# Scan decays: the running sums' rows fetched from memory as broadcasts and masked by GpSimd, instead of being spread and masked by matmuls

## The chip, the cores and the metric

The kernel runs on one core of a Trainium2 chip. The metric is the device time of one execution in microseconds (us), lower is better; three executions of the kernel before gave a median of 1445.81 us.

## The reference, cut to what matters

The kernel is one inference step of a two-layer backbone in float32. Layer 0 has differential attention beside a bidirectional state-space scan (SSD); layer 1 has a pooling mixer; both end in an MLP of width 4096. The change touches the scan of layer 0 alone. For one direction and one chunk of q = 128 tokens it computes

```python
acs = jnp.cumsum((dt * a).reshape(nb, nc, q, H), axis=2)
seg = acs[:, :, :, None, :] - acs[:, :, None, :, :]
causal = jnp.tril(jnp.ones((q, q), bool))[None, None, :, :, None]
decay = jnp.where(causal, jnp.exp(jnp.where(causal, seg, 0.0)), 0.0)
cb = jnp.einsum('bclhn,bcshn->bclsh', ch, bh) * decay
y_diag = jnp.einsum('bclsh,bcshp->bclhp', cb, xdt)
```

There are 5 chunks (4 of the 512 latent tokens, 1 of the 128 prompt tokens), 2 directions and 8 heads in 2 groups. The backward direction uses the opposite triangle.

## The kernel before, in words

The program is written engine by engine; semaphores are the only order between engines. Every engine runs its own list strictly in order, so an instruction that waits holds back all that stands behind it on that engine. Matmuls in the big projections are split into high and low halves (three products for one).

The part that matters is the loop `for j in range(2 * NT)` of layer 0, ten rounds, here called rounds 0 to 9. Each round of TensorE (PE) holds, in this order: one projection of 24 matmuls (`project_in`, L801), the decay matmuls (`decays`, L1008 and L1010), two transposes of a query or key block (`turn_qk`, L949), in even rounds 8 matmuls of a modulation product (`site`, L832), the products of the weighted pairs of the round before with the values (`chunk_y(j - 1)`, L1031), and the pair products C·B of this round (`pair_products(j)`, L1020). A pair u is one chunk and one group of four heads: u = 0 to 9.

For a pair u the decays are made so. The cumulated sums `acs` were transposed once to rows and multiplied with a small pick matrix into `acsr` (L2206). PE writes, for each direction, a bank of 128 x 512: first the triangle mask (0 or -1e30, from `maskr`, four times side by side, L1008), then it adds the rows of `acsr`, spread over all 128 partitions by a picking matmul (L1010). ScalarE (ACT) takes eight exponentials of 128 x 128 from PSUM, with the other sum as bias, into `seg[u % 2]` (L1541). VectorE (DVE) adds the two directions (L2158) and multiplies with the pair products (L2161, `weigh_pairs(u)`, semaphore `m_ok`). PE's `chunk_y(u)` waits for that; its end is the semaphore `yd_mm`.

DVE's list in round j is: `weigh_pairs(j - 1)`, `evac_in` of this round's projection (L2125 and L2134, or copies), in rounds 3 and 9 the low half of the next weight block (`split_lo`, L1926), in even rounds from 2 on `chunk_sum` (L2167, L2170). PE's first projection after the loop waits for the `split_lo` of round 9. GpSimd (POOL) has nothing to do in these rounds: it waits for the last `evac_in` to store two outputs (L645). It issues many of the kernel's DMAs and does small powers (L617, L720, L727).

Earlier, at the start, POOL loads small tables (L625 to L629, `ssd_c` holds the two triangles and the two masks, L628); ACT waits for all five, copies them (L1487 to L1490) and only then evacuates the first convolution input (L1507).

## Time and profile before

| | |
|---|---|
| median of 3 runs | 1445.81 us (1445.0 to 1446.02) |
| span of the profiled execution | 1442.8 us |
| PE busy | 1397.0 us (97%) |
| DVE busy | 1040.2 us (72%) |
| ACT busy | 543.1 us (38%) |
| POOL busy | 77.3 us (5%) |

The span is that of the one profiled execution, first to last instruction; the median of the timed runs lies 3.0 us above it. Busy time of PE is pipelined: a matmul of 256 columns is shown with about 280 ns although the next one starts 120 ns later, so what a group of matmuls costs is read from the starts of the groups, not from the busy time.

### The profile page before, as it was taken

To read this page: it belongs to the slowest core of one execution; us is meant where nothing else is said; L and a number is where in the kernel's file an instruction comes from. 1 tells how busy PE (TensorE), PEld (TensorE's weight loads), DVE (VectorE), ACT (ScalarE), POOL (GpSimd) and SP (SyncE) were. 2 spreads that over 40 slices of the span, in tenths; PEclk is the share of its full clock that TensorE was granted. 3 is DMA by queue.
4 is the path that set the end of the run, shared out by engine and by line. 5 is a ranking of instruction groups with operands and counts; after the bars stand their busy time and mean duration, and the time that the engine had idled before them with its cause. 6 is when DMAs were issued, how large, how long until landed. Compare 5 with 4: busy or idle time off the path is not lost.

```text
span 1442.8 us, 22837 instructions
## 1 busy us (share of the span) xinstructions
PE 1397.0 (97%) x8806; PEld 1240.1 (86%) x8806; DVE 1040.2 (72%) x1651; ACT 543.1 (38%) x982; POOL 77.3 (5%) x146
## 2 busy tenths in 40 slices
PE   4999999999999999999999999999999999999996
PEld 3899988766779998998899879888999889989985
DVE  3694566777568876776776796877887677667778
ACT  4333343367454332332232254434443223223322
POOL 1300000010201000000000111001000000000011
PEclk9999999999999999999999999999999999999998
DMA  9701234696713312321221723551332122123141
GB/s 316 232 30 60 88 118 133 213 310 228 265 45 137 126 59 83 94 87 59 87 88 58 268 88 114 185 185 37 146 103 85 62 88 88 59 87 116 59 160 73
DMA packets 132300, 177.47 MB, mean 123 GB/s; under 512 B 4170, under 2 KB 104258, under 8 KB 131698
## 3 DMA queue, kind: packets, MB, share of 16 engines
q1 hardware_dynamic: 123250, 146.46, 31.4%
q0 software_dynamic: 7376, 26.76, 5.3%
q10 hardware_dynamic: 1584, 3.01, 0.6%
q8 instruction: 61, 1.00, 0.3%
q14 instruction: 29, 0.24, 0.0%
HBM read 166.94 MB, written 9.27 MB: 122 GB/s over the span
## 4 chain that ended last, share of the span: by engine, by line
PE 79%; DVE 10%; ACT 5%; issue 2%; DMA 2%; SPq 1%; POOL 0%; ACTq 0%; DVEq 0%
PE ps L801 40%; PE ps L1325 20%; PE ps L783 5%; PE ps L792 4%; PE ps L832 2%; DVE convT L2024 2%; PE ps L1133 2%; DVE wlo L1926 1%; ACT h_full L1722 1%; SPq L570 1%; DVE p_pad L2691 1%; DMA raw_more<-in_w_mod_l 1%; ACT tmp L1722 1%; ACT whi L1430 1%; PE ps L1144 1%
## 5 line engine op out<-in xcount | busy, mean ns | idle before, releaser
L1430 ACT ACTIVATE whi<-raw 128x512 fp32r<-128x512 f32 (+2 forms) x193 | 178.6, 935 | 357.8 <-PE ps L801 293.6
L801 PE MATMUL ps<-whi,hid_hi 128*128 128x512 f32 x640 | 249.6, 390 | 0.0
L801 PE MATMUL ps<-wlo,hid_hi 128*128 128x512 f32 x640 | 249.2, 389 | 0.0
L801 PE MATMUL ps<-whi,hid_lo 128*128 128x512 f32 x640 | 249.1, 389 | 0.0
L1926 DVE TENSOR_TENSOR wlo<-raw,whi 128x512 fp32r<-128x512 f32 (+2 forms) x193 | 204.9, 1070 | 26.0 <-ACT whi L1430 22.5
L2357 DVE TENSOR_TENSOR acc<-acc,ps 128x512 f32<-128x512 f32 x120 | 80.2, 684 | 122.0 <-PE ps L801 122.0
L801 PE MATMUL ps<-whi,h_hi 128*128 128x256 f32 (+1 forms) x480 | 157.4, 328 | 2.5 <-DVE wlo L1926 1.4
L801 PE MATMUL ps<-whi,h_lo 128*128 128x256 f32 (+1 forms) x480 | 152.9, 319 | 0.0
L801 PE MATMUL ps<-wlo,h_hi 128*128 128x256 f32 (+1 forms) x480 | 152.8, 318 | 0.0
L801 PEld LDWEIGHTS ps<-whi,hid_hi 128*128 128x128 f32 x640 | 120.1, 188 | 25.4 <-DVE wlo L1926 0.8
L801 PEld LDWEIGHTS ps<-whi,hid_lo 128*128 128x128 f32 x640 | 120.1, 188 | 25.1
L801 PEld LDWEIGHTS ps<-wlo,hid_hi 128*128 128x128 f32 x640 | 120.1, 188 | 24.2
L1325 PE MATMUL ps<-t_hi,whi 128*128 128x320 f32 x384 | 118.7, 309 | 0.0
L1325 PE MATMUL ps<-t_hi,wlo 128*128 128x320 f32 x384 | 118.7, 309 | 0.0
L1325 PE MATMUL ps<-h_lo,whi 128*128 128x320 f32 x384 | 118.6, 309 | 0.0
L1325 PE MATMUL ps<-h_hi,whi 128*128 128x320 f32 x384 | 118.2, 309 | 0.0
L2497 DVE TENSOR_TENSOR tmp<-tmp,ps 128x320 f32<-128x320 f32 x168 | 79.2, 483 | 37.2 <-PE ps L1325 33.1
L801 PEld LDWEIGHTS ps<-whi,h_hi 128*128 128x128 f32 x480 | 91.2, 190 | 10.3 <-DVE wlo L1926 2.0
L801 PEld LDWEIGHTS ps<-whi,h_lo 128*128 128x128 f32 x480 | 91.2, 190 | 6.5
L801 PEld LDWEIGHTS ps<-wlo,h_hi 128*128 128x128 f32 x480 | 91.4, 190 | 5.9
L1325 PE MATMUL ps<-h_hi,wlo 128*128 128x320 f32 x288 | 89.0, 309 | 0.0
L783 PE MATMUL ps<-h_hi,whi 128*128 128x320 f32 x320 | 73.4, 310 | 0.0
(339 smaller groups left out, 2654.6 us busy)
## 6 DMA issues: line engine op xcount, KB each, us to landing
raw<-in_w_up_l SPq DMA_DIRECT2D x32, 1024.0 KB, 5.6
raw<-in_w_down_l SPq DMA_DIRECT2D x32, 1024.0 KB, 4.9
raw<-in_w_mod_l SPq DMA_DIRECT2D x26, 1024.0 KB, 5.8
raw<-in_w_in_l SPq DMA_DIRECT2D x12, 1024.0 KB, 5.2
raw_split<-in_w_mod_l SPq DMA_DIRECT2D x8, 1024.0 KB, 6.7
raw<-in_w_out_l SPq DMA_DIRECT2D x6, 1024.0 KB, 5.9
x_spill<-x_tok POOLq DMA_DIRECT2D x10, 512.0 KB, 2.9
x_tok<-x_spill POOLq DMA_DIRECT2D x10, 512.0 KB, 6.2
```

What stands on the lines that cost most here:

```text
L783: mm = pe.matmul(outs[hf], w_of(still, k), a_of(part, k, hf), start=(k == 0 and part == 0 and still == 0), stop=(k == nk - 1 and still == 1))
L792: mm = pe.matmul(out, w_of(still, k), a_of(part, k, hf), start=(k == 0 and part == 0 and still == 0), stop=(k == nk - 1 and still == 1))
L801: mm = pe.matmul(out, a_of(still, k), w_of(part, k), start=(first and k == 0 and part == 0 and still == 0), stop=(last and k == nk - 1 and ...
L832: mm = pe.matmul(ps[32 * g:32 * g + 32, lo:lo + BW], cpad[:, k, :], raw_block(mod_k[m])[:, k * BW:(k + 1) * BW], start=(k < 4), stop=(k >= 4))
L1133: mm = pe.matmul(bank(2 * n + part, 0, keys.shape[-1]), qT[r:r + DH, 2 * n + hp, t * P:(t + 1) * P], keys, start=True, stop=True)
L1325: mm = pe.matmul(bank(b, 0, HALF), WP[still][:, pos // 4, lo:lo + P], moving(part, k), start=(k == 0 and still == 0 and part == 0), stop=( ...
L1430: act.activation(ring_piece(whi, w, g), piece(w, g), ACT.Copy).then_inc(hi_done, 1)
L1722: ins = act.activation(dst, bank(TURN[i % 2][t][f // 4], (f % 4) * P, (f % 4 + 1) * P), ACT.Identity, bias=modT[:, layer, q, f, c:c + 1], ...
L1926: dve.tensor_tensor(ring_piece(wlo, w, g), piece(w, g), ring_piece(whi, w, g).bitcast(F32), ALU.subtract).then_inc(lo_done, 1)
L2024: ins = dve.scalar_tensor_tensor(dst, src, tap, dst, ALU.mult, ALU.add)
L2357: dve.tensor_tensor(dst, dst, bank(4 + g % 4), ALU.add).then_inc(acc_ok, 1)
L2497: dve.tensor_tensor(dst, a, bank(b, 0, HALF), ALU.add).then_inc(comb, 1)
```

## The change

The four decay matmuls of each round, the masks in `maskr`, the pick matrices and `acsr`'s product are gone. In their place the transposed sums (one transpose and one copy, `acsr` is now 80 x 128) are stored once to memory (`acs_rows`). POOL fetches for each pair the four rows of each direction, broadcast to all 128 partitions, straight into `seg[u % 3]` (512 KB, now three buffers), and puts -1e30 outside the triangle with one `affine_select` of 128 x 512 for each direction (semaphore `tri_ok`). ACT then takes the same eight exponentials in place, from `seg` and no longer from PSUM. The table `t_ssd` shrinks from four to two blocks of 128 x 128, so its load and ACT's copy of it are half as large, and the copy of the identity is gone. DVE has five small instructions less at the sums and one copy for two products.

```diff
+            def fetch_rows(u):
+
+                first = 8 * ORDER[u // 2] + 4 * (u % 2)
+                if u >= 3:
+                    pool.wait_ge(yd_mm, u - 2)
+                rows = A["acs_rows"][:, first:first + 4, :].rearrange("d h n -> d (h n)")
+                pool.dma_start(seg[u % 3][:].rearrange("p d h n -> p d (h n)"), rows.partition_broadcast(P)) \
+                    .then_inc(seg_ld[u % 3], 16)
+
+            def triangle(u):
+
+                pool.wait_ge(seg_ld[u % 3], 16 * (u // 3 + 1))
+                for d in range(2):
+                    side = 1 - 2 * d
+                    pool.affine_select(seg[u % 3][:, d], seg[u % 3][:, d], [[0, 4], [side, P]], ALU.is_ge, NEG,
+                                       base=0, channel_multiplier=-side).then_inc(tri_ok, 1)
+
+            pool.wait_ge(acs_ok, 4)
+            pool.dma_start(A["acs_rows"].rearrange("d h n -> (d h) n"), acsr[0:80]).then_inc(rows_st, 16)
+            pool.wait_ge(rows_st, 16)
+            for u in range(2):
+                fetch_rows(u)
+            for u in range(2 * NT):
+                if u + 2 < 2 * NT:
+                    fetch_rows(u + 2)
+                triangle(u)
...
-            def decays(u):
-
-                c, g = ORDER[u // 2], u % 2
-                for d in range(2):
-                    if u >= 1:
-                        pe.wait_ge(eexp, 2 * (u - 1) + d + 1)
-                    else:
-                        pe.wait_ge(acs_ok, 3)
-                        pe.wait_ge(xb_ev, KT)
-                    pe.matmul(bank(d), maskr[:, 4, :], maskr[:, 2 + d, :].unsqueeze(1).to_broadcast([P, 4, P]),
-                              start=True, stop=False)
-                    pe.matmul(bank(d), pickr[0:80, 2 * c + g:2 * c + g + 1].to_broadcast([80, P]), acsr[0:80, d, :],
-                              start=False, stop=True).then_inc(r_mm, 1)
...
-            act.activation(maskr[:, 0:4, :], ssdc[:], ACT.Copy)
-            act.activation(maskr[:, 4, :], ident, ACT.Copy).then_inc(mask_ok, 1)
+            act.activation(maskr[:], ssdc[:], ACT.Copy).then_inc(dt_w, 1)
...
             def decays(u):
 
                 c, g = ORDER[u // 2], u % 2
-                if u >= 2:
-                    act.wait_ge(yd_mm, u - 1)
                 for d in range(2):
-                    act.wait_ge(r_mm, 2 * u + d + 1)
+                    act.wait_ge(tri_ok, 2 * u + d + 1)
                     for h in range(4):
-                        ins = act.activation(seg[u % 2][:, d, h, :], bank(d, h * P, (h + 1) * P), ACT.Exp,
+                        ins = act.activation(seg[u % 3][:, d, h, :], seg[u % 3][:, d, h, :], ACT.Exp,
                                              bias=nacs[:, d, c, 4 * g + h:4 * g + h + 1])
                     ins.then_inc(eexp, 1)
```

How the built programs stand, at the two places that matter. First POOL's list between the loads of the start and the stores of outputs, before; `kc`, `rope_t`, `state_ld` and `v_tok` are loads of the start, `out` are stores:

```order
L635 DMA rope_t_98<-in_t_rope 128x256
L637 DMA state_ld_111<-in_state_ssm_l0 128x4x128 x2
L640 DMA v_tok_90<-in_cache_v_l0 128x512 x2
L645 DMA out_2<-tmp_67 128x256 x2
L647 DMA out_3<-v_tok_90 128x512
```

The same place in the changed program; `acs_rows_102` is the tile, `acs_rows` the tensor in memory, and seg0, seg1 and seg2 are the three buffers:

```order
L632 DMA state_ld_109<-in_state_ssm_l0 128x4x128 x2
L635 DMA v_tok_90<-in_cache_v_l0 128x512 x2
L656 DMA acs_rows<-acs_rows_102 80x128
L644 DMA seg0_104<-acs_rows 128x2x512
L644 DMA seg1_105<-acs_rows 128x2x512
L644 DMA seg2_106<-acs_rows 128x2x512
L652 ISA
L652 AFFINE_SELECT seg0_104<-seg0_104 128x512 x2
L644 DMA seg0_104<-acs_rows 128x2x512
L652 AFFINE_SELECT seg1_105<-seg1_105 128x512 x2
L644 DMA seg1_105<-acs_rows 128x2x512
L652 AFFINE_SELECT seg2_106<-seg2_106 128x512 x2
```

The fetch into a buffer stands ahead of the selects of another buffer: the fetch of pair 3 (second row of seg0's DMA) waits for `chunk_y(0)`, and behind it stand the selects of pair 1, and so on in every round.

Second, PE's list in round 2, before, from the end of the projection to the first matmuls of the next:

```order
L801 MATMUL ps<-whi_57,h_lo_61 128x256
L1008 MATMUL ps<-mask_r_100 128x512
L1010 MATMUL ps<-acs_rows_102,pick_r_105 128x512
L1008 MATMUL ps<-mask_r_100 128x512
L1010 MATMUL ps<-acs_rows_102,pick_r_105 128x512
L949 MATMUL ps<-head_68,tmp_67 128x128 x2
L832 MATMUL ps<-raw_49,cpad_69 32x256 x8
L1031 MATMUL ps<-xb_tok_99,seg1_108 128x64 x4
L1020 MATMUL ps<-convT_86 128x128
L801 MATMUL ps<-whi_57,h_hi_60 128x256
```

And in the changed program:

```order
L822 MATMUL ps<-whi_57,h_lo_61 128x256
L970 MATMUL ps<-head_68,tmp_67 128x128 x2
L853 MATMUL ps<-raw_49,cpad_69 32x256 x8
L1035 MATMUL ps<-xb_tok_99,seg1_105 128x64 x4
L1024 MATMUL ps<-convT_86 128x128
L822 MATMUL ps<-whi_57,h_hi_60 128x256
```

The four decay matmuls are gone; all else on PE keeps its place.

## Rows read from the trace of the kernel before

**Rows 1.** The page: busy time of PE, and the chain by engine.

```profile
PE 1397.0 (97%) x8806; PEld 1240.1 (86%) x8806; DVE 1040.2 (72%) x1651; ACT 543.1 (38%) x982; POOL 77.3 (5%) x146
PE 79%; DVE 10%; ACT 5%; issue 2%; DMA 2%; SPq 1%; POOL 0%; ACTq 0%; DVEq 0%
```

**Rows 2.** Busy time by stretch: stretch, length, engines, granted clock, DMA share, GB/s.

```profile
169.50:221.40 51.90, 51.90 (x436) 46.03 (x435) 31.23 (x70) 27.05 (x88) 0.00 (x0) 1.00 0.38 122
20.00:30.00 10.00, 6.12 (x77) 3.08 (x76) 6.53 (x16) 6.00 (x9) 0.00 (x0) 1.00 1.10 348
```

**Rows 3.** Timeline of PE in rounds 1, 8, 9: start, duration, what.

```profile
174.99 0.39 PE L1008 MATMUL ps<-mask_r 128*128 128x512 f32 x1
175.94 0.38 PE L949 MATMUL ps<-head,tmp 128*128 128x128 f32 x2
176.16 1.00 PE L1031 MATMUL ps<-xb_tok,seg 128*128 128x64 f32 x8
...
216.94 1.10 PE L1031 MATMUL ps<-xb_tok,seg 128*128 128x64 f32 x8
...
222.20 1.00 PE L1031 MATMUL ps<-xb_tok,seg 128*128 128x64 f32 x8
...
228.93 1.10 PE L1031 MATMUL ps<-xb_tok,seg 128*128 128x64 f32 x8
```

**Rows 4.** Timeline of ACT, round 0.

```profile
171.18 2.17 ACT L1541 ACTIVATE seg<-ps,ssd_small 128x128 f32<-128x128 f32 x8
```

**Rows 5.** Timeline of DVE, rounds 0 to 9, in brackets its wait before.

```profile
173.38 0.69 DVE L2158 TENSOR_TENSOR seg<-seg 128x512 f32<-128x512 f32 x1 [2.37 <-ACT seg L1541]
174.11 0.69 DVE L2161 TENSOR_TENSOR seg<-seg,ps 128x512 f32<-128x512 f32 x1
...
180.35 0.75 DVE L2125 TENSOR_TENSOR tmp<-ps,rope_t 128x256 f32<-128x256 f32 x2
181.13 0.49 DVE L2134 TENSOR_TENSOR tmp<-tmp 128x128 f32<-128x128 f32 x2
181.87 0.69 DVE L2167 TENSOR_TENSOR y_tok<-xb_tok,dsk 128x512 f32<-128x512 f32 x1 [0.24 <-DVE tmp L2134]
...
222.30 2.29 DVE L1926 TENSOR_TENSOR wlo<-raw,whi 128x2048 fp32r<-128x2048 f32 x1 [0.24 <-DVE tmp L2118]
```

**Rows 6.** Groups of POOL: busy time, mean ns of one, idle before.

```profile
L740 POOL DMA_DIRECT2D x_tok<-x_spill x10 | 5.2, 529 | 651.0 <-PE ps L1325 651.0
L622 POOL MEMSET conv_raw<- 128x1296 f32 x1 | 1.2, 1178 | 11.2 <-DVE cpad L1979 11.2
L605 POOL MEMSET cpad<- 128x256 f32 x1 | 0.3, 311 | 0.3 <-POOLq L2749 0.3
```

**Rows 7.** Timeline of POOL beside DVE, at the norms of layer 0.

```profile
412.25 0.69 DVE L2346 SCALAR_TENSOR_TENSOR x_tok<-x_tok,gated 128x512 f32<-128x512 f32 x1
...
412.36 0.63 POOL L727 TENSOR_TENSOR ln_small<-ln_small 128x1 f32<-128x1 f32 x1
415.47 0.19 POOL L727 TENSOR_TENSOR ln_small<-ln_small 128x1 f32<-128x1 f32 x1
```

**Rows 8.** The chain that ended last, pieces in order of time.

```profile
47.11 1.04 PE ps L832 x16
48.44 0.91 POOL wdt L625
...
51.25 5.44 DMA dsk<-in_d_skip_l
57.12 0.52 ACT mask_r L1489
```

**Rows 9.** Timeline of ACT at the table copies.

```profile
57.03 0.61 ACT L1489 ACTIVATE mask_r<-ssd_c 128x512 fp32r<-128x512 f32 x1
57.55 0.29 ACT L1490 ACTIVATE mask_r<-head 128x128 fp32r<-128x128 f32 x1
57.75 0.42 ACT L1507 ACTIVATE conv_raw<-ps 128x320 f32<-128x320 f32 x1
```

**Rows 10.** DMA issues: size of one, median us to landing.

```profile
x_tok<-x_spill POOLq DMA_DIRECT2D x10, 512.0 KB, 6.2
ln_gb<-in_ln_b_l POOLq DMA_DIRECT2D x4, 512.0 KB, 9.4
```

More of the change, by code:

```diff
@@ L234, in build @@
         cdec = rend
-        seg = [at(f"seg{n}", kb, [P, 2, 4, P]) for n, kb in enumerate((172, 186))]
+        seg = [at(f"seg{n}", kb, [P, 2, 4, P]) for n, kb in enumerate((172, 186, 168))]
         kc = at("kc", 176, [P, 2, 2, 4, DH])
@@ L293, in build @@
             ("xb_mm", "xb_ev", "cv_v", "cv_th", "cv_ok"))
-        ld_dt, ld_kc, ld_st, v_ev, mask_ok = (sem(n) for n in
-            ("ld_dt", "ld_kc", "ld_state", "v_ev", "mask_ok"))
+        ld_dt, ld_old, v_ev = (sem(n) for n in ("ld_dt", "ld_cache_state", "v_ev"))
         dt_w, dt_wl, dt_row, dt_cp, dt_mm, dt_v, dt_ok = (sem(n) for n in
@@ L301, in build @@
             ("xt_tr", "xt_ev", "acs_mm", "acs_ok", "kc_tr", "kc_ev", "sld_tr", "hst_ok"))
-        r_mm, g_mm, eexp, m_ok, yd_mm, y_ok = (sem(n) for n in
-            ("r_mm", "g_mm", "e_exp", "m_ok", "yd_mm", "y_ok"))
-        dec_s, dec_e, w_ok, off_mm, st_mm, off_ok, h_ok = (sem(n) for n in
-            ("dec_s", "dec_e", "ws_ok", "off_mm", "st_mm", "off_ok", "hs_ok"))
+        rows_st, g_mm, eexp, tri_ok, m_ok, yd_mm, y_ok = (sem(n) for n in
+            ("acs_rows_st", "g_mm", "e_exp", "triangle_ok", "m_ok", "yd_mm", "y_ok"))
+        seg_ld = [sem(f"seg_ld{n}") for n in range(3)]
+        dec_e, w_ok, off_mm, st_mm, off_ok, h_ok = (sem(n) for n in
+            ("dec_e", "ws_ok", "off_mm", "st_mm", "off_ok", "hs_ok"))
         nst_tr, nst_ev, yg_ok, yg_sq, yg_rs, yn_ok = (sem(n) for n in
@@ L982, in turn_sums @@
                 pe.wait_ge(acs_ok, 1)
-                for d in range(2):
-                    mm = pe.transpose(ps[0:80, 7 * 512 + 256 + P * d:7 * 512 + 256 + P * (d + 1)],
-                                      achl[:, d, :].bitcast(F32), ident)
-                mm.then_inc(acs_mm, 1)
+                pe.transpose(ps[0:80, 7 * 512 + 256:7 * 512 + 256 + P], sm[:, 80:160], ident).then_inc(acs_mm, 1)
             todo = [M_MIX]
@@ L997, in site @@
                     site_product()
-            def decays(u):
-                c, g = ORDER[u // 2], u % 2
-                for d in range(2):
-                    if u >= 1:
-                        pe.wait_ge(eexp, 2 * (u - 1) + d + 1)
-                    else:
-                        pe.wait_ge(acs_ok, 3)
-                        pe.wait_ge(xb_ev, KT)
-                    pe.matmul(bank(d), maskr[:, 4, :], maskr[:, 2 + d, :].unsqueeze(1).to_broadcast([P, 4, P]),
-                              start=True, stop=False)
-                    pe.matmul(bank(d), pickr[0:80, 2 * c + g:2 * c + g + 1].to_broadcast([80, P]), acsr[0:80, d, :],
-                              start=False, stop=True).then_inc(r_mm, 1)
             def pair_products(u):
@@ L1030, in chunk_y @@
                     cols = slice((4 * g + h) * DH, (4 * g + h + 1) * DH)
-                    mm = pe.matmul(bank(3, cols.start, cols.stop), seg[u % 2][:, 0, h, :], xb[:, ORDER[n], cols],
+                    mm = pe.matmul(bank(3, cols.start, cols.stop), seg[u % 3][:, 0, h, :], xb[:, ORDER[n], cols],
                                    start=True, stop=True)
@@ L2086, in _ @@
             settle()
[L2087 to L2093 removed]
+            dve.wait_ge(acs_ok, 1)
             mark(dve.tensor_tensor(dtw, rend, acs, ALU.subtract))
@@ L2097, in _ @@
             settle()
-            dve.nop().then_inc(dec_s, 1)
+            dve.nop().then_inc(acs_ok, 1)
             def evac_in(g):
@@ L2204, in _ @@
                     dve.wait_ge(acs_mm, 2)
-                    for d in range(2):
-                        ins = dve.tensor_tensor(acsr[0:80, d, :].rearrange("p (h n) -> p h n", h=4),
-                                                ps[0:80, 7 * 512 + 256 + P * d:7 * 512 + 256 + P * (d + 1)]
-                                                .unsqueeze(1).to_broadcast([80, 4, P]),
-                                                pick[0:80, 10:14].unsqueeze(2).to_broadcast([80, 4, P]), ALU.mult)
-                        if d == 0:
-                            mark(ins)
-                    ins.then_inc(acs_ok, 1)
+                    dve.tensor_copy(acsr[0:80], ps[0:80, 7 * 512 + 256:7 * 512 + 256 + P]).then_inc(acs_ok, 1)
             for j in range(2 * NT):
```

43 lines of the change are left out of this document (14 added, 29 removed).

## The prediction, made before the changed kernel ran

> **What bounds the kernel now.** I read the page first: PE is busy 97% of the span and makes up 79% of the chain that ended last [rows 1]. Then the busy time by stretch: from 169.5 to 221.4 us, which is the loop that the change edits but for its last round, PE is busy 51.90 of 51.90 us at a granted clock of 1.00, the 2.4 GHz level, while DVE is busy 31.2, ACT 27.1 and POOL not at all [rows 2]. So a microsecond taken from PE's list there is a microsecond of the kernel, until something else ends last. Last I read the timeline for the pace of the rounds and for what lies between one `chunk_y` and the next.
>
> **The rounds before.** The decay matmuls of a round take 175.94 - 174.99 = 0.95 us on PE [rows 3]. `chunk_y(0)` starts at 176.16 and `chunk_y(7)` at 216.94, seven rounds of 5.83 us on the mean; `chunk_y(8)` follows at 222.20 and `chunk_y(9)` at 228.93 [rows 3]. If nothing but PE mattered, ten times 0.95 us would go, 9.5 us.
>
> **What the new order makes of it.** POOL's list decides. Behind the fetch for pair u + 2 stand the selects of pair u, and that fetch waits for `chunk_y(u - 1)`, because it overwrites the buffer that this one reads. The selects of pair u need nothing from `chunk_y(u - 1)`, yet cannot pass the fetch. So for u = 1 to 7 there is a closed loop: `chunk_y(u - 1)`, issue of a fetch, select, eight exponentials, two DVE products, `chunk_y(u)`. Before, the exponentials of pair u ran while PE worked on the same round, ahead of `chunk_y(u - 1)`; two buffers let them. Fetches 8 and 9 are the last ones, so the selects of pairs 8 and 9 follow at once.
>
> One turn of the loop, from start to start of `chunk_y`:
> - `chunk_y` itself 1.00 [rows 3];
> - PE's end to POOL's start 0.29: the modulation product ends at 47.11 + 1.04 = 48.15 and POOL starts at 48.44 [rows 8];
> - issue of the fetch 0.57: a 512 KB load is issued in 0.53 [rows 6], a little more for two pieces per partition;
> - the first select, T (below);
> - to ACT 0.10, an estimate like the small gaps around it;
> - eight exponentials 2.17 [rows 4]; the last four need the second select, which is hidden while T is under 1.04 (half of 2.17, less the pipeline's tail);
> - to DVE 0.04 and the two products 1.42: 171.18 + 2.17 = 173.35, start 173.38, end 174.11 + 0.69 = 174.80 [rows 4, 5];
> - to PE 0.10, an estimate.
>
> Without T this is 5.69 us. It is already 0.14 short of a round of before.
>
> **The select.** No row has one. A memset takes 311 ns for 256 elements of a partition and 1178 for 1296 [rows 6]: 0.83 ns an element and 0.10 us fixed. At that rate 512 elements take 0.53 us, which is the bound below, since a select also reads, counts an index and compares. I take two such rates, 0.95 us. Three rates give 1.38 and four 1.81; above that no row leads. GPSIMD Engine Reference, section 3.1, of the Trainium skill gives 1.8 cycles at 1.2 GHz per element for a tight loop and 2.6 with two inputs; the estimate from that page would be 0.77 to 1.11 us for 512 elements, and the sum below would change by -1.3 to +1.6 us. No row here shows such a loop.
>
> **Seven turns.** L = 5.69 + 0.95 = 6.64 us. `chunk_y(0)` starts two decay groups earlier, at 176.16 - 1.90 = 174.26; its exponentials are not late, since both first fetches have 20 us. `chunk_y(7)` then starts at 174.26 + 7 x 6.64 = 220.74 in place of 216.94: **+3.8 us**. PE idles some 1.5 to 2.5 us in every round.
>
> **DVE in POOL's way.** An operation of POOL that reads a tile was held while DVE ran one with two tile inputs: the same L727 takes 0.19 us alone and 0.63 beside L2346, and ends 0.05 after it [rows 7]. The Trainium skill has it as a rule (SBUF — State Buffer, section "SBUF: two separate sides"): the two share a port pair, one that starts first keeps it for the whole instruction. The trace agrees, with that 0.63. Here the select of pair u would start 0.10 + 1.00 + 0.29 + 0.57 = 1.96 us after `m_ok` of the pair before. DVE runs `evac_in` until 1.3, and after a settle of 0.24 the L2167 of even rounds from 1.54 to 2.23 [rows 5]: 0.27 us in each of rounds 2, 4 and 6, 0.8 in all. In round 3 `split_lo` of 2.29 us stands there, from 1.54 to 3.83 [rows 5]: 1.87 us once. Together **+2.7 us**; nothing, if selects are not held.
>
> **The end of the loop.** Round 8 has selects that wait for nothing, so PE goes at its own pace: 5.26 - 0.95, and some 0.2 of waiting, 4.5 us in place of 5.26 [rows 3]. Behind `chunk_y(8)` the pair's DVE work is now late and `split_lo` of round 9 with it: from `m_ok` on some 0.85 for `evac_in` (two copies here, an estimate; 1.27 at most, as in round 2 [rows 5]), 0.24, 2.29, and from the end of `split_lo` to `chunk_y(9)` the 228.93 - 224.59 = 4.34 of before [rows 3, 5]; less the 0.1 from `m_ok` to `chunk_y(8)` that is 7.6 us in place of 228.93 - 222.20 = 6.73. Sum of both **+0.1 us**.
>
> **The start.** The chain runs through the table loads: the last of them lands 5.44 us after its issue, ACT copies, and DVE's convolution follows [rows 8]. ACT's two mask copies take 57.75 - 57.03 = 0.72 us [rows 9]. Afterwards one of 256 columns is left, about 0.31: **-0.4 us**. The halved table may save a little of the landing (0 to 0.3). The one transpose less at the sums is **-0.1 us** of PE. DVE's saved products (some 2 us) lie in rounds where DVE waits for PE: nothing.
>
> **What costs nothing while its cover holds.** A fetch is issued two turns, 13 us, ahead of its select; loads of 512 KB from POOL land in 6.2 to 9.4 us [rows 10], at a DMA share of 0.38 [rows 2]. If they took 16, each turn would grow by about 1.5 us, and the loop would be 10 us longer. The state transposes that now wait for one semaphore less were not late. The granted clock stayed at 1.00 in a stretch where PE was busy 6.12 of 10 us [rows 2], so idling a third of a round should leave it.
>
> **Sum.** 3.8 + 2.7 + 0.1 - 0.4 - 0.1 = +6.1 us. On the profiled execution's own 1442.8 that is 1448.9. The median of the runs lies 3.0 above that span; the same shift gives 1445.8 + 6.1 = **1451.9 us**.
>
> **Rivals.**
> - *The select is long* (T over 1.04). Then the second select sets the exponentials and L = 4.65 + 2T. At three memset rates that is 7.41, `chunk_y(7)` at 226.1, +9.2 in the loop and about +11.5 in all, 1457.3 us; at four rates 8.27 and 1463.3. For it: the select does at least three things where memset does one. Against it: it is one input and one output.
> - *No change.* T is 0.53 and selects are not held: L = 6.22, seven turns end at 217.8, +0.9, less 0.4 at start, end and sums: 1446.3 us. For it: memset's rate. Against it: the held L727.
> - *Faster.* The loop closes, but the exponentials read a tile instead of PSUM and follow each other faster: a copy of 128 x 128 from a tile is followed by the next instruction after 0.20 us [rows 9], an exponential now after about 0.26 [rows 4]. Eight of them save 0.46 a turn. With T = 0.53 and no holding L is 5.76 and the kernel takes 1443.0 us. Without holding, the sign turns at L = 6.15. Full PE pace, 4.9 us a round and 1435.8, would need another 0.9 us off every turn.
> - *A fetch that lands late*, as above: about 1462 us. Against it: 13 us of lead.
>
> **How the numbers follow.** Chances: the loop with a select of 0.53 to 1.04 us and held selects 0.55, the long select 0.21, no change 0.14, faster 0.07, late fetches 0.03. A measurement of this kernel can tell 0.2%, 2.9 us. The two slow rivals and the forecast make slower 0.79; "no change" is same, 0.14; faster is 0.07. The forecast's own span is 1449.0 (T 0.53, held) to 1452.5 (T 1.04, held); the range reaches down to the no-change case and up to a select of nearly four rates: 1445.5 to 1461.
>
> **What would show it.** In the changed profile: L1008 and L1010 gone; PE idle before L1035 in rounds 2 to 8 with DVE's `m_ok` product as releaser, 1 to 3 us each; starts of L1035 6.6 us apart instead of 5.2 and 6.4 in turn; the largest gap in round 4, behind `split_lo`'s round; POOL waiting for L1035 ahead of each fetch; the select's own length; none of PE's idle time released by a DMA. I am wrong if rounds are 4.3 and 5.3 us long (then something lets the selects run ahead), if selects take 0.5 us and don't care about DVE, or if they take over 1.4.

## The result, and the profile of the changed kernel

The changed kernel takes 1455.09 us in the median of four runs (1453.82 to 1456.1). The kernel before, run beside it, takes 1445.4 us (four runs, 1443.83 to 1446.02). The ratio is 1.0069, with an interval of 1.0057 to 1.0081: slower by 9.7 us. The profiled execution has a span of 1454.2 us, against 1442.8.

The page of the changed kernel, busy time and chain, as in [rows 1]:

```profile
PE 1397.4 (96%) x8765; PEld 1242.0 (85%) x8765; DVE 1039.8 (72%) x1645; ACT 545.5 (38%) x981; POOL 99.5 (7%) x177
PE 74%; DVE 10%; issue 6%; ACT 5%; DMA 2%; SPq 1%; POOL 1%; ACTq 0%; DVEq 0%; POOLq 0%
```

PE has 41 matmuls less, yet is shown busy as long as before, and its share of the chain fell from 79% to 74%. The busy time by stretch says why, over the same stretch as in [rows 2], then over the rest of the loop, one piece of it, and a piece of layer 1. The columns are stretch, length, busy time of PE, PEld, DVE, ACT and POOL, granted clock, DMA share, GB/s:

```profile
169.50:221.40 51.90, 41.97 (x332) 38.29 (x322) 25.45 (x56) 23.59 (x74) 16.41 (x23) 0.88 0.53 171
221.40:242.00 20.60, 17.82 (x139) 15.79 (x139) 12.67 (x24) 10.56 (x28) 3.34 (x6) 0.88 0.54 170
...
218.00:221.00 3.00, 3.00 (x16) 3.00 (x16) 0.00 (x0) 1.06 (x4) 2.47 (x4) 0.50 0.31 85
1000.00:1040.00 40.00, 37.30 (x224) 34.56 (x224) 29.12 (x47) 23.90 (x51) 3.78 (x7) 0.96 0.25 80
```

Where PE was busy 51.90 of 51.90 us at a clock of 1.00, it is now busy 41.97 us, at 0.88. Both are losses: PE waits, and part of what it does runs at the lower level, 1.2 GHz, which is the 0.50 of the third row.

The timeline of PE, all starts of `chunk_y` but three, with PE's wait before in brackets (in the changed file `chunk_y` is L1035, the projection L822):

```profile
173.55 1.02 PE L1035 MATMUL ps<-xb_tok,seg 128*128 128x64 f32 x8
180.25 1.10 PE L1035 MATMUL ps<-xb_tok,seg 128*128 128x64 f32 x8 [1.31 <-DVE seg L2153]
187.03 1.10 PE L1035 MATMUL ps<-xb_tok,seg 128*128 128x64 f32 x8 [2.31 <-DVE seg L2153]
...
216.25 1.97 PE L1035 MATMUL ps<-xb_tok,seg 128*128 128x64 f32 x8 [2.68 <-DVE seg L2153]
224.71 1.10 PE L1035 MATMUL ps<-xb_tok,seg 128*128 128x64 f32 x8
229.02 1.00 PE L1035 MATMUL ps<-xb_tok,seg 128*128 128x64 f32 x8
...
232.41 0.39 PE L822 MATMUL ps<-whi,h_hi 128*128 128x256 f32 x1 [2.11 <-DVE wlo L1924]
...
238.20 1.10 PE L1035 MATMUL ps<-xb_tok,seg 128*128 128x64 f32 x8
```

I call turn k the time from the start of `chunk_y(k-1)` to that of `chunk_y(k)`. The nine turns are 6.70, 6.78, 8.16, 6.77, 7.14, 7.15, 8.46, 4.31 and 9.18 us. Before, the first seven made 40.78 and the last two 11.99 us [rows 3]; now they make 51.16 and 13.49.

One turn through the engines, timelines of POOL, ACT and DVE. L644 is the fetch, L652 the two selects, L1539 the eight exponentials, L2150 and L2153 the two products:

```profile
174.87 0.73 POOL L644 DMA_DIRECT2D seg<-acs_rows  x1 [17.62 <-PE ps L1035]
175.61 1.24 POOL L652 TENSOR_SCALAR_AFFINE_SELECT seg<-seg 128x512 f32<-128x512 f32 x2
```

```profile
176.30 0.70 ACT L1539 ACTIVATE seg<-seg,ssd_small 128x128 f32<-128x128 f32 x2 [2.17 <-POOL seg L652]
...
177.78 0.97 ACT L1539 ACTIVATE seg<-seg,ssd_small 128x128 f32<-128x128 f32 x3
```

```profile
178.78 0.69 DVE L2150 TENSOR_TENSOR seg<-seg 128x512 f32<-128x512 f32 x1 [3.97 <-ACT seg L1539]
179.51 0.69 DVE L2153 TENSOR_TENSOR seg<-seg,ps 128x512 f32<-128x512 f32 x1
```

Read in order of time, each link starts within 0.1 us of the end of the one that it needs, from `chunk_y(0)` (ends 174.57) to `chunk_y(1)` (180.25), except POOL's start, 0.30 behind PE's end: issue to 175.60, first select (half of 1.24) to 176.23, exponentials to 178.75, products to 180.20. But for the second select, which runs under the first exponentials, nothing in this circle overlaps with anything else in it. The waits of the loop, in total, times, longest, give the same circle:

```profile
POOL seg L644 <- PE ps L1035: 47.7, 7, 17.6
ACT seg L1539 <- POOL seg L652: 26.4, 7, 4.7
DVE seg L2150 <- ACT seg L1539: 25.8, 8, 4.9
...
PE ps L1035 <- DVE seg L2153: 9.8, 5, 2.7
```

Last, the two places where POOL and DVE met: round 3 with `split_lo` (L1924), and round 6 with L2159, which takes 0.69 us elsewhere, as L2167 did in [rows 5]:

```profile
188.41 2.29 DVE L1924 TENSOR_TENSOR wlo<-raw,whi 128x2048 fp32r<-128x2048 f32 x1 [0.24 <-DVE tmp L2126]
...
210.62 1.16 DVE L2159 TENSOR_TENSOR y_tok<-xb_tok,dsk 128x512 f32<-128x512 f32 x1 [0.24 <-DVE tmp L2129]
```

```profile
189.17 2.62 POOL L652 TENSOR_SCALAR_AFFINE_SELECT seg<-seg 128x512 f32<-128x512 f32 x2
...
211.24 1.62 POOL L652 TENSOR_SCALAR_AFFINE_SELECT seg<-seg 128x512 f32<-128x512 f32 x2
```

Two selects take 1.24 us alone, 2.62 beside `split_lo` and 1.62 in round 6, where the DVE product beside them is 0.47 longer as well.

### The profile page after: what moved, and what is told of

It reads as the page before. It is cut to its first block, busy times and chain, and to the rows that moved or that the text cites. A ratio compares the mean times of both kernels' runs of the same rounds, so it can differ in the third digit from the quotient of the medians.

```text
span 1454.2 us, 22789 instructions
## 1 busy us (share of the span) xinstructions
PE 1397.4 (96%) x8765; PEld 1242.0 (85%) x8765; DVE 1039.8 (72%) x1645; ACT 545.5 (38%) x981; POOL 99.5 (7%) x177
## 4 chain that ended last, share of the span: by engine, by line
PE 74%; DVE 10%; issue 6%; ACT 5%; DMA 2%; SPq 1%; POOL 1%; ACTq 0%; DVEq 0%; POOLq 0%
PE ps L822 37%; PE ps L1326 20%; PE ps L804 5%; PE ps L813 4%; PE ps L853 2%; DVE convT L2022 2%; PE ps L1134 2%; DVE wlo L1924 1%; ACT h_full L1720 1%; SPq L565 1%; DVE p_pad L2676 1%; DMA raw_more<-in_w_mod_l 1%; ACT tmp L1720 1%; ACT whi L1431 1%; PE ps L1145 1%
## 5 line engine op out<-in xcount | busy, mean ns | idle before, releaser
L822 PE MATMUL ps<-whi,hid_hi 128*128 128x512 f32 x640 | 249.6, 390 | 0.0
L822 PE MATMUL ps<-wlo,hid_hi 128*128 128x512 f32 x640 | 249.1, 389 | 0.0
L822 PE MATMUL ps<-whi,hid_lo 128*128 128x512 f32 x640 | 249.1, 389 | 0.0
L1924 DVE TENSOR_TENSOR wlo<-raw,whi 128x512 fp32r<-128x512 f32 (+2 forms) x193 | 204.9, 1070 | 26.0 <-ACT whi L1431 22.5
L822 PE MATMUL ps<-whi,h_hi 128*128 128x256 f32 (+1 forms) x480 | 160.4, 334 | 2.9 <-DVE wlo L1924 2.4
L822 PE MATMUL ps<-whi,h_lo 128*128 128x256 f32 (+1 forms) x480 | 155.6, 324 | 0.0
L822 PE MATMUL ps<-wlo,h_hi 128*128 128x256 f32 (+1 forms) x480 | 155.5, 324 | 0.0
L822 PEld LDWEIGHTS ps<-whi,hid_hi 128*128 128x128 f32 x640 | 120.1, 188 | 25.3 <-DVE wlo L1924 0.8
L822 PEld LDWEIGHTS ps<-whi,hid_lo 128*128 128x128 f32 x640 | 120.1, 188 | 25.2
L822 PEld LDWEIGHTS ps<-wlo,hid_hi 128*128 128x128 f32 x640 | 120.2, 188 | 24.2
L822 PEld LDWEIGHTS ps<-whi,h_hi 128*128 128x128 f32 x480 | 94.3, 197 | 10.8 <-DVE wlo L1924 3.0
L822 PEld LDWEIGHTS ps<-whi,h_lo 128*128 128x128 f32 x480 | 94.0, 196 | 6.5
L822 PEld LDWEIGHTS ps<-wlo,h_hi 128*128 128x128 f32 x480 | 94.4, 197 | 5.8
```

Of the source, the lines that this page charges most:

```text
L822: mm = pe.matmul(out, a_of(still, k), w_of(part, k), start=(first and k == 0 and part == 0 and still == 0), stop=(last and k == nk - 1 and ...
L1924: dve.tensor_tensor(ring_piece(wlo, w, g), piece(w, g), ring_piece(whi, w, g).bitcast(F32), ALU.subtract).then_inc(lo_done, 1)
```

## The experiments

Each stands against the kernel before, run beside it. Where an experiment edits the kernel after, its time is also compared with that kernel's 1455.1 us.

### Fetch one pair ahead: is it the loop?

If the selects of pair u stand behind the wait for `chunk_y(u - 2)` and not for `chunk_y(u - 1)`, there is no closed loop of one round, with the same instructions and buffers.

```diff
-            for u in range(2):
+            for u in range(3):
                 fetch_rows(u)
             for u in range(2 * NT):
-                if u + 2 < 2 * NT:
-                    fetch_rows(u + 2)
+                if 3 <= u + 1 < 2 * NT:
+                    fetch_rows(u + 1)
                 triangle(u)
```

> Edit: GpSimd fetches only one pair ahead inside the loop, so the selects of pair u stand behind the wait for chunk_y(u-2), not behind the one for chunk_y(u-1). Nothing is left out. Theory A (a closed loop: the selects of a pair are issued behind the wait for the pair before it, and every round hangs on chunk_y, fetch issue, selects, exponentials, products): the loop is cut, the rounds go at TensorE's own pace of 4.3 and 5.3 us, no idle time over 0.5 us is left ahead of L1035 in the middle of the loop, the granted clock there is 1.00, and the time is 1435 to 1438 us (ratio to before 0.993 to 0.995). Theory B (the chain of a round is too long in any order, or the landing of a fetch, 4.4 us in the middle, now comes late, since it is asked for only one round ahead): TensorE still waits 1 us or more in most rounds and the time is 1448 us or more. Theory C (only the dip of the clock costs): rounds still 6.6 us apart, time as after, 1454 to 1456 us.

Measured: 1438.42 us (1437.43 to 1440.09), before 1445.57, ratio 0.9955 [0.9942, 0.9969]. That is 16.7 us less than the kernel after, by the order of POOL's list alone. PE's timeline, some starts of `chunk_y` and the wait of the last projection:

```profile
173.73 1.02 PE L1035 MATMUL ps<-xb_tok,seg 128*128 128x64 f32 x8
179.05 1.10 PE L1035 MATMUL ps<-xb_tok,seg 128*128 128x64 f32 x8
183.36 1.00 PE L1035 MATMUL ps<-xb_tok,seg 128*128 128x64 f32 x8
188.97 1.10 PE L1035 MATMUL ps<-xb_tok,seg 128*128 128x64 f32 x8 [0.24 <-DVE seg L2153]
...
213.00 1.00 PE L1035 MATMUL ps<-xb_tok,seg 128*128 128x64 f32 x8
...
216.39 0.39 PE L822 MATMUL ps<-whi,h_hi 128*128 128x256 f32 x1 [2.11 <-DVE wlo L1924]
...
222.14 1.10 PE L1035 MATMUL ps<-xb_tok,seg 128*128 128x64 f32 x8
```

The turns are 5.32 and 4.31 us one after the other, which is the pace of before (6.25 and 5.25, with `chunk_y(1)` at 182.41 and `chunk_y(2)` at 187.66) less the 0.95 us of decay products; only turns 3, 6 and 7 are longer, at 5.61, 4.70 and 5.40. The last is 9.14, and PE's waits ahead of `chunk_y` are 0.24 at most. The busy time by stretch, again over the stretch of [rows 2], and over the last round:

```profile
169.50:221.40 51.90, 49.32 (x440) 44.83 (x436) 37.75 (x75) 32.36 (x98) 19.59 (x26) 0.97 0.68 225
...
215.00:222.00 7.00, 5.61 (x42) 4.80 (x42) 2.75 (x4) 1.57 (x6) 0.82 (x2) 0.76 0.70 225
```

Theory A stands, with a time 0.4 us above what it said (1438.4 where 1435 to 1438 was said). The clock fell only where PE still waited: 0.76 in the last round, behind the 2.11 us for `split_lo`. The landing is no longer hidden entirely, since POOL's selects now wait for a fetch for 9.2 us in all (3.8 in the kernel after), but none of it reaches PE.

### The selects twice: dose and response

```diff
-                    pool.affine_select(seg[u % 3][:, d], ...).then_inc(tri_ok, 1)
+                    pool.affine_select(seg[u % 3][:, d], ...).then_inc(ss_, 1)
+                    steps[0] += 1
+                    pool.wait_ge(ss_, steps[0])
+                    pool.affine_select(seg[u % 3][:, d], ...).then_inc(tri_ok, 1)
```

> Edit: each of the two selects of a pair is done twice (the second changes nothing), with a wait for the first between. Theory A (the selects stand in the loop that sets the round's length): each round is longer by two selects of 0.62 to 0.65 us and two waits of about 0.1 us less what runs under the exponentials (the second direction's select can lie under the first direction's exponentials of 1.2 us): 0.7 to 1.4 us a round over seven to eight rounds, so 5 to 11 us more than after: 1460 to 1466 us, ratio to before 1.010 to 1.014. Theory B (GpSimd's selects are off the path, and what costs is the exponentials, the products of VectorE or TensorE's clock): no more than 1 us on 1455 us.

Measured: 1463.24 us (1461.77 to 1466.17), ratio 1.0122 [1.0107, 1.0138], 8.1 us over the kernel after. The groups of the two selects of a direction, busy time and mean ns of one, and PE at `chunk_y(1)`, here L1039:

```profile
L652 POOL TENSOR_SCALAR_AFFINE_SELECT seg<-seg 128x512 f32<-128x512 f32 x20 | 14.6, 730 | 2.6 <-DMA seg<-acs_rows 2.5
L656 POOL TENSOR_SCALAR_AFFINE_SELECT seg<-seg 128x512 f32<-128x512 f32 x20 | 13.1, 657 | 2.9
```

```profile
181.25 1.97 PE L1039 MATMUL ps<-xb_tok,seg 128*128 128x64 f32 x8 [2.29 <-DVE seg L2157]
```

The first turn, from `chunk_y(0)` at 173.58, grew from 6.70 to 7.67 us: one more select and its wait, and little of the second direction's, which lies under exponentials. POOL is busy 7% of the span, and yet what it does once more in each round, every round pays. Not all of the 8.1 us is the selects' own time: `chunk_y(1)` takes 1.97 us here in place of 1.10, at the lower clock (0.62 from 180 to 185 us). Theory A.

### The same dose where the loop is cut

The doubled selects of the last edit, in the order of the first. This one tells a loop from a mere shortage of time on POOL.

> Edit: each select done twice, as in the run before, on the version with fetches one pair ahead. Theory A (a closed loop, which that order cuts): the doubled selects, which cost 8 us in the other order, now have some 1 us of room in each round and cost 0 to 2 us: 1438 to 1440.5 us. Theory B (that order gained by something else, and the selects are still on the path): 6 us or more on 1438.4 us: 1444 us or more.

Measured: 1441.51 us (1438.91 to 1442.81), ratio 0.997 [0.9959, 0.9982]: 3.1 us over the single selects, where the closed loop paid 8.1. Through `chunk_y(5)` nothing moved (turns of 5.3, 4.3, 5.6, 4.3 and 5.3 us). Then POOL, which had waited for a landing in round 5, was late once:

```profile
204.65 1.31 PE L1039 MATMUL ps<-xb_tok,seg 128*128 128x64 f32 x8 [1.49 <-DVE seg L2157]
```

POOL had waited 3.06 us for that landing, and then had eight selects to do, with one fetch between. That turn is 5.96 us in place of 4.70, and the next 6.94 in place of 5.40, with the granted clock at 0.89 from 200 to 215 us. Theory A is right in kind, and its 0 to 2 us were too few: the cut loop has not the slack for four selects in every round.

### TensorE kept busy: what the clock costs

Products whose results nothing reads, in two placings: four in every round, and three or four only where PE waits.

```diff
+            def filler(n):
+                for k in range(n):
+                    pe.matmul(bank(k % 2), maskr[:, 0, :], maskr[:, 1, :].unsqueeze(1).to_broadcast([P, 4, P]),
+                              start=True, stop=True)
             for j in range(2 * NT):
                 project_in(4 * NT + j)
+                if 2 <= j < 9:
+                    filler(3)
...
                 pair_products(j)
+                if j == 9:
+                    filler(4)
```

(The run with filler in every round has its four products, unconditionally, behind `project_in`.)

> Edit: four products of 128 x 512 whose results nothing reads are put on TensorE behind the projection of each round, where the decay products stood before the change. TensorE's queue in a round grows by some 0.9 us of work that lies in the time in which it waits for chunk_y's release. Theory A (TensorE's idle time lets the granted clock fall, and the clock costs 3 to 4 us of the 9.3 that the loop loses): granted clock over 0.95 through the loop, rounds still 6.6 to 6.8 us apart, time 1450 to 1452.5 us. Theory B (the clock's dip costs nothing beyond the waits, since TensorE waits anyway): 1454 to 1456 us as after. Theory C (the filler stands in the way of the release): over 1457 us.

> Edit: on the kernel after the change, three products of 128 x 512 whose results nothing reads in rounds 2 to 8, just behind the projection, and four in round 9 behind the pair products, where TensorE waits for the split weights: in its waiting time alone, unlike the filler of all rounds, which cost 1.6 us in rounds 0 and 1. Theory A (the granted clock falls because TensorE waits, and this costs 3 to 4 us in the loop): chunk_y(0) at 173.6 as after, turns of rounds 4 and 5 6.8 us instead of 7.14, turns of 8 and 9 together at least 1.5 us shorter, granted clock above 0.9 in the middle; time 1451 to 1452.5 us. Theory B (the filler's gain in the loop was another thing's): turns as after, time 1454.5 us or more.

Measured: in every round 1453.96 us (1453.2 to 1455.14), ratio 1.0059 [1.0045, 1.0073]; in the waits alone 1452.93 us (1451.95 to 1453.26), ratio 1.0053 [1.004, 1.0066]. So more work on the bounding engine makes the kernel no slower, and in the waits alone 2.2 us faster than the kernel after, whose fastest execution (1453.82) is slower than the slowest here (1453.26). The 1.1 us of the other placing is not clear of noise: its executions and those of the kernel after overlap. The busy time by stretch, filler in the waits:

```profile
169.50:221.40 51.90, 43.52 (x358) 38.68 (x355) 25.68 (x57) 24.79 (x77) 16.61 (x23) 0.97 0.54 174
221.40:242.00 20.60, 18.75 (x157) 16.12 (x157) 14.64 (x26) 9.56 (x24) 3.06 (x5) 1.00 0.56 179
1000.00:1040.00 40.00, 37.30 (x238) 34.98 (x237) 30.44 (x45) 24.92 (x48) 3.53 (x7) 1.00 0.27 93
```

The clock is 0.97 and 1.00 where it was 0.88 and 0.88; it is low only in turn 7, at 0.80 from 215 to 220 us. Turn by turn: 5 from 7.14 to 6.78, 7 from 8.46 to 7.60, 9 from 9.18 to 7.69; the others are as they were within 0.01 us. Together 2.7 us, and `chunk_y(7)` to `chunk_y(9)` takes 11.99 us, to the hundredth what it took before the change. Theory A has its mechanism, and its time was half a microsecond optimistic; of the filler in every round I had said 1450 to 1452.5, and it missed by 1.5 because four products in rounds 0 and 1, where PE does not wait, cost 1.6 us (`chunk_y(0)` at 175.19), and its clock still fell to 0.78 and 0.83 in places.

### Writing the exponentials elsewhere

The eight exponentials take 2.45 us, 2.17 before [rows 4], with more space between starts: (2.45 - 0.39) / 7 = 0.29 us against (2.17 - 0.36) / 7 = 0.26. Reading moved from PSUM to a tile; reading and writing are in one tile now. The edit sends direction 1's output to a bank of PSUM:

```diff
+                    if d == 1 and u >= 1:
+                        act.wait_ge(m_ok, u)
                     for h in range(4):
-                        ins = act.activation(seg[u % 3][:, d, h, :], seg[u % 3][:, d, h, :], ACT.Exp,
+                        ins = act.activation(seg[u % 3][:, 0, h, :] if d == 0 else bank(1, h * P, (h + 1) * P),
+                                             seg[u % 3][:, d, h, :], ACT.Exp,
...
-                mark(dve.tensor_tensor(s[:, 0], s[:, 0], s[:, 1], ALU.add))
+                mark(dve.tensor_tensor(s[:, 0], s[:, 0], bank(1).rearrange("p (h n) -> p h n", h=4), ALU.add))
```

> Edit: the exponentials of direction 1 are written to a PSUM bank instead of in place, and VectorE's sum of the two directions reads them there. Nothing is left out. It parts the reading from the writing in the eight exponentials, which take 2.44 us from and to the tile where they took 2.17 us from PSUM to a tile before. Theory A (reading a tile in SBUF is what makes the spacing 0.30 instead of 0.26 us): direction 1's four stay at 0.30 us, time as after within 1.5 us. Theory B (reading and writing the same buffer, or writing SBUF while VectorE and GpSimd use it, is what costs): direction 1's spacing is 0.26 us or less, 0.15 us a round, time 1453 to 1454.5 us. VectorE's sum from PSUM may be some tenths of a us longer or shorter than 0.69 us in either case; this adds to each round of the loop.

Measured: 1453.37 us (1452.34 to 1455.4), ratio 1.0059 [1.0045, 1.0073]. ACT's timeline, four exponentials to the tile, four to PSUM:

```profile
182.72 1.28 ACT L1541 ACTIVATE seg<-seg,ssd_small 128x128 f32<-128x128 f32 x4 [4.02 <-POOL seg L652]
183.91 1.23 ACT L1541 ACTIVATE ps<-seg,ssd_small 128x128 f32<-128x128 f32 x4
```

and the groups by shape, mean ns of one behind the busy time:

```profile
L1541 ACT ACTIVATE seg<-seg,ssd_small 128x128 f32<-128x128 f32 x40 | 12.8, 390 | 24.8 <-POOL seg L652 24.8
L1541 ACT ACTIVATE ps<-seg,ssd_small 128x128 f32<-128x128 f32 x40 | 12.3, 351 | 0.0
```

The spacing is (1.23 - 0.35) / 3 = 0.29 us into PSUM and (1.28 - 0.39) / 3 = 0.30 into the tile: the same. Only each one's end comes 0.04 us sooner. So it is not the place written that spaces them, and what differs from before is the place read: theory A, by exclusion. No run reads PSUM and writes the tile in this loop, so that the place read is the cause is argued and not shown. The Trainium skill (ScalarE: Activation LUTs, section "Step-by-step: what each stage is for") calls PSUM ScalarE's lower-latency port as a destination; the trace agrees, with 351 against 390 ns, and in this loop that is worth 0.04 us a turn. The time, 1.7 us less, lies in the range of theory B and not of A, so by the time alone B would stand. But 0.04 us in each of seven turns makes 0.3 us. Most of the rest of the profiled execution's gain stands in turns 5 and 7 (6.74 and 6.91 us, 7.14 and 8.46 in the kernel after), where the clock cost less, and the last experiment has the same without this edit.

### `split_lo` in quarters: who holds whom

```diff
-                if j in (3, 9):
-                    split_lo(9 + j // 8)
+                if j == 3:
+                    split_parts(9)    # four dve.tensor_tensor of 128 x 512 in place of one of 128 x 2048
+                if j == 9:
+                    split_lo(10)
```

> Edit: on the kernel after the change, VectorE's subtraction of 128 x 2048 in round 3 (2.29 us), during which GpSimd's two selects took 2.62 us instead of 1.24, is done as four of 128 x 512. Nothing is left out. Theory A (an instruction of the one engine holds one of the other until it ends, so the selects get in between the pieces): the two selects take 2.0 us or less, the turn of 8.16 us shrinks by 0.5 to 1.2 us, and the time by as much: 1453.9 to 1454.6 us (1453.4 if the clock's dip behind it goes too). Theory B (a select that lies beside VectorE's work is slow or kept out for as long as VectorE has anything to do): 2.6 us again or more, and the time is 1455 to 1455.5 us. Four pieces cost VectorE some 0.2 to 0.4 us more than one.

Measured: 1453.86 us (1449.14 to 1454.7), ratio 1.0055 [1.0043, 1.0067]. DVE's and POOL's timelines in round 3:

```profile
188.56 3.75 DVE L1934 TENSOR_TENSOR wlo<-raw,whi 128x512 fp32r<-128x512 f32 x4 [0.24 <-DVE tmp L2137]
```

```profile
189.32 1.23 POOL L652 TENSOR_SCALAR_AFFINE_SELECT seg<-seg 128x512 f32<-128x512 f32 x2
```

and the least, middle and greatest duration (ns) of the four pieces:

```profile
L1934 DVE TENSOR_TENSOR wlo<-raw,whi x4: 677/686/1934, 188.6 to 191.6; 128x512 fp32r<-128x512 f32 x4
```

The selects take 1.23 us again, and now it is DVE that is held: three pieces take 0.68 us and one 1.93, longer by 1.25, which is the two selects. Turn 3 is 6.89 us in place of 8.16. Theory A, by the turn's 1.27 us. The time alone could not show it: it is 1.2 us less than the kernel after, 0.95 if each is taken against the kernel before that ran beside it, and the executions (1449.14 to 1454.7) overlap with those of the kernel after. The Trainium skill (SBUF — State Buffer, section "SBUF: two separate sides") has whichever of the two starts first keep the shared ports for its whole instruction, and the other block. The kernel after agrees in round 3: `split_lo` starts at 188.41, and the first select, from 189.17, takes 2.03 us and ends 0.50 behind it. Here the rows do not agree:

```profile
189.17 1.93 DVE L1934 TENSOR_TENSOR wlo<-raw,whi 128x512 fp32r<-128x512 f32 x1
189.32 0.65 POOL L652 TENSOR_SCALAR_AFFINE_SELECT seg<-seg 128x512 f32<-128x512 f32 x1
```

The piece that was held starts 0.15 us ahead of the first select, and it was held over both selects and not over one. Which of the two engines gives way at such a meeting is left open by these runs.

### The split ahead of the evacuation: a faster version

In the cut loop PE's last long wait is the 2.11 us for `split_lo` of round 9, which stands on DVE behind an evacuation that nothing needs so soon.

```diff
             for j in range(2 * NT):
                 if j >= 1:
                     weigh_pairs(j - 1)
+                if j == 9:
+                    split_lo(10)
                 evac_in(4 * NT + j)
-                if j in (3, 9):
-                    split_lo(9 + j // 8)
+                if j == 3:
+                    split_lo(9)
```

> Edit: on the version with fetches one pair ahead, VectorE's split of the weights for the last projection of the loop stands before the evacuation of round 9, not behind it. In that version TensorE still waits 2.11 us there, for that split, and the granted clock is 0.78 behind it. Theory A (the wait is for the order on VectorE, and the clock falls because of the wait): the split starts some 1.4 us earlier (GpSimd's cache rows and the next transposes wait 2.3 us longer for the copies, under 3 us of projection), the wait shrinks to under 1 us, the clock stays at 1.00, and of the last turn of 9.14 us 1.4 to 2.8 us go: 1435.6 to 1437 us. Theory B (what is won is lost to the transposes of the keys, which now come late): 1438 us or more.

> Edit: on the kernel before the change, VectorE's split of the weights for the last projection of the loop stands before the evacuation of round 9, as in the fastest version so far. It tells how much of that version's lead over the kernel before is the fetched decays' and how much the split's. Theory A (TensorE's wait of 1.16 us there is for the order on VectorE): it goes, 1443.9 to 1444.6 us, so that the fetched decays in a cut loop are worth 8 us of the 9.2. Theory B (the clock, 1.00 there, has nothing to give and the moved split makes the copies for the transposes late): 1445 us or more.

Measured on the cut loop: 1435.92 us (1435.19 to 1437.44), ratio 0.9934 [0.9921, 0.9947]. It is the fastest kernel of the study, 9.2 us under the kernel before. PE at the last projection, and the last round's stretch:

```profile
215.37 0.39 PE L822 MATMUL ps<-whi,h_hi 128*128 128x256 f32 x1 [0.70 <-DVE wlo L1924]
```

```profile
215.00:222.00 7.00, 6.28 (x58) 5.29 (x58) 4.57 (x10) 2.67 (x9) 1.67 (x3) 1.00 0.74 241
```

The wait shrank to 0.70, the clock stayed at 1.00 where it had been 0.76, and the last turn is 6.27 us in place of 9.14. Of these 2.87 us, 1.41 are the shorter wait; the other 1.46 go with the clock, as much again. (The filler took as much, 1.49 us, off the same turn of the closed loop.) Theory A.

Measured on the kernel before: 1444.81 us (1442.02 to 1445.65), against 1444.91, ratio 0.9992 [0.9983, 1.0001]. The trace has the effect, in PE's timeline:

```profile
222.37 1.00 PE L1031 MATMUL ps<-xb_tok,seg 128*128 128x64 f32 x8
227.68 1.10 PE L1031 MATMUL ps<-xb_tok,seg 128*128 128x64 f32 x8
```

The last turn is 5.31 us in place of 6.73 [rows 3], PE's wait of 1.16 us is gone, and yet the medians differ by 0.1 us. The interval takes in both theories. So how much of the fastest version's 9.2 us the fetched decays brought is known from the first experiment (7.2 us), not from this one.

### The copies put back: where the start's gain is from

```diff
-            act.activation(maskr[:], ssdc[:], ACT.Copy).then_inc(dt_w, 1)
+            act.activation(maskr[:], ssdc[:], ACT.Copy)
+            act.activation(unread[:, 0:2, :], ssdc[:], ACT.Copy)
+            act.activation(unread[:, 2, :], ident, ACT.Copy).then_inc(dt_w, 1)
```

> Edit: on the kernel after the change, ScalarE copies three more blocks of 128 x 128 (two of the table, the identity) into a tile that nothing reads, where the five-block copy of the masks stood before; the load of the table stays half as large. It parts the two sources of the start's gain (the convolution's first product on VectorE at 57.67 us, 58.59 before; first projection of the loop's stage at 106.49, 107.11 before; chunk_y(0) at 173.55). Theory A (ScalarE's copies, as in the prediction): the gap from the first copy to the first evacuation of the convolution is 0.7 to 0.8 us instead of 0.30, and VectorE's first product and all behind it come 0.4 to 0.5 us later than in the kernel after: chunk_y(0) at 173.9 to 174.1. Theory B (the smaller and earlier table load): all within 0.1 us of the kernel after: chunk_y(0) at 173.5 to 173.7. One look: the time itself can't tell half a microsecond.

Measured, in a single run: 1454.29 us. DVE's first product of the convolution:

```profile
58.35 0.87 DVE L2023 TENSOR_SCALAR convT<-conv_raw,vecT 128x512 f32<-128x512 f32 x2 [1.23 <-ACT conv_raw L1512]
```

From ACT's first mask copy to its first evacuation it is 0.82 us, where it was 0.30 in the kernel after and 0.72 before. DVE's product comes 0.68 later, at 58.35; 0.18 of that is not the copies, since ACT itself starts on them later (its first copy at 56.38 against 56.20), behind a load that nothing edited. The first projection comes only 0.19 later (106.68 against 106.49) and `chunk_y(0)` 0.19 (173.74 against 173.55), between the two theories. Neither holds as said. The copies delay the chain's beginning by 0.5 us, but whether any of it reaches the loop can't be told: the eight profiles of this study with the start of the kernel after have `chunk_y(0)` anywhere from 173.24 to 174.14.

This run shows something else. Its loop is the loop of the kernel after, word for word, and turns 5 and 7 differ. The starts of `chunk_y(6)` and `chunk_y(7)`:

```profile
216.08 1.10 PE L1036 MATMUL ps<-xb_tok,seg 128*128 128x64 f32 x8 [2.68 <-DVE seg L2156]
222.97 1.10 PE L1036 MATMUL ps<-xb_tok,seg 128*128 128x64 f32 x8
```

Turn 7 is 6.89 us, not 8.46, and turn 5 6.79, not 7.14, behind the same wait of 2.68 us ahead of `chunk_y(6)`; the granted clock is 0.93 and 0.92 over the two stretches, not 0.88 and 0.88. So what the clock takes in those two turns varies from one execution to the next, and that is about the 1.8 us by which this execution is shorter than the profiled one of the kernel after (spans of 1452.4 and 1454.2).

## Why the prediction was right, and where its steps were off

Direction, mechanism and range held: 1455.1 in 1445.5 to 1461, forecast 1451.9. It was 3.2 us short. The steps below are read from the profiled execution, which was the slowest of the four (1456.1). There the forecast span of 1448.9 was 5.3 us short: 3.2 by `chunk_y(9)` and 2.1 after the loop. The median lies 0.9 us above this span and lay 3.0 above that of before, and that difference takes the 2.1 away again. By its own steps:

- **The closed loop.** As said, link by link, and shown by the first two experiments and their pairing: the same selects, doubled, cost 8.1 us in the closed loop and 3.1 in the cut one, and the order alone is worth 16.7.
- **One turn, 6.64 us.** Measured 6.70 and 6.78, but by errors that cancel. The select takes 0.62, not 0.95, nearly the lower bound that I had from memset and did not take (-0.33). The exponentials take 2.45, not 2.17 (+0.28): the forecast kept the duration from PSUM, and its "faster" rival had them shorter still, from a copy's row. The issue of a fetch in two pieces per partition takes 0.72, not 0.57 (+0.15). The gaps are 0.03 to 0.07 us, not 0.10 (-0.1). From turn 2 on `chunk_y` itself is 1.10 (+0.1). Seven turns without holding or clock make 6.70 + 6 x 6.78 = 47.4, forecast 46.5.
- **Selects held by DVE, +2.7.** The mechanism is right (`split_lo` in quarters), the size was too big: 1.38 us in round 3, 0.37 in round 6, nothing in rounds 2 and 4, 1.8 in all. With the issue 0.15 longer, the selects start at 182.39, 0.07 behind the end of the product that was to hold them (181.63 + 0.69).
- **The clock, "idling a third of a round should leave it".** This is the step that failed. In the profiled execution it cost 0.36 us in turn 5, 1.68 in turn 7 and 1.49 in turn 9, 3.5 in all; the filler took back 2.7 of it. In the execution with the copies put back turns 5 and 7 lost 0.1 us together and turn 9 again 1.5, so the whole term was 1.6 there: the loss in turn 9 came in each execution of the closed loop that was profiled without filler, from turn to turn in the middle it did not. (In turn 7 nothing is waited for ahead of `chunk_y(7)`: PE's own list, at 0.50 from 218 to 221 us, sets its end.) I had argued from a stretch in which PE was busy 6.12 of 10 us at 1.00 [rows 2], at the start of the kernel; it did not carry over to here. Seven turns +0.9, holding -0.9 and clock +3.5 make the error up to the loop's end, with -0.2 at the start and -0.1 in the last two turns. How much of the median's 3.2 us is the clock isn't known as closely.
- **The end of the loop, +0.1.** Right but for the clock: 13.49 us where 11.99 were before, and 11.99 with the filler.
- **The start, -0.4, and the sums, -0.1.** `chunk_y(0)` came at 173.55, forecast 174.26 - 0.5 = 173.76. The size is right as far as can be told, since `chunk_y(0)` lies anywhere from 173.24 to 174.14 with the same start, and its reason is not shown: the copies put back moved it by 0.19 us, less than that spread. The half-size table load was not tried by itself; ACT began its copies at 56.71 before and at 56.20 in the kernel after, but anywhere from 56.07 to 56.75 in the experiments with the half-size table.
- **After the loop.** The difference of the profiled executions is 9.27 us at `chunk_y(9)` and 11.4 at the end. Of the 2.1 between, 1.5 stand in layer 1, between 1000 and 1040 us, where PE waits as long as before (1.87 us against 1.86, then 0.60 against 0.62) but from the first wait to the second it is 13.81 us and was 12.29, and the clock is 0.96 and was 1.00. The filler in the waits has 1.00 there again, though nothing of it was edited there. The waits are the same where it falls and where it doesn't; what decides it stays open, and no run isolated it.
- **The rivals.** The long select is out (0.62 us). "No change" and "faster" needed a shorter turn; the select was as short as they asked, and the exponentials took it back. Full pace of PE, which I had priced at 1435.8 us and called out of reach by 0.9 us a turn, was met by the order instead, at 1435.9, but partly by luck: that version also has the split moved, which the price did not hold, and without it it takes 1438.4. The paces of before, told as 5.2 and 6.4 us, are 5.25 and 6.25 by the trace; nothing in the sum rests on them. No fetch came late in the kernel after but the one for pair 9, by 1.1 us, and PE did not feel it.

## What to carry to other kernels

Before work goes to an idle engine, write its list out in order and ask of each wait which later instruction stands behind it without needing it. Here an engine busy 7% of the time set the pace of the one busy 97%, because a refill two ahead waited for this round's reader and the next round's mask stood behind the refill. A prefetch distance is not free when it shares a queue with the work: fetching one pair ahead instead of two turned a loss of 0.7% into a gain of 0.45%. And a wait on TensorE is to be priced with what the granted clock does behind it: in the loop's last round that was as much again as what the wait shrank by.
